# The expert stage of a mixture-of-experts step in native float32, on 32-column token tiles

## The reference

```python
aff = softmax(h @ w_router); gate, idx = top_k(aff, cap)     # per expert: 64 and 16 tokens
xs = h[idx]                                                  # 80 rows of 1024
hid = silu(xs @ w_gate[e]) * (xs @ w_up[e])                  # 1024 -> 2816
out = (hid @ w_down[e]) * gate                               # 2816 -> 1024
acc[idx] += out                                              # scatter-add, then x += gate2 * acc
```

## Time and profile before

| what | us |
|---|---|
| median of 3 runs (lowest, highest) | 2162.31 (2161.64, 2163.51) |
| the profiled execution's own time | 2162.86 |
| its span in the trace | 2161.0 |
| PE busy in the span | 2107.8 (98%) |
| DVE busy | 1598.9 (74%) |
| ACT busy | 1333.8 (62%) |
| DMA over the span | 646.76 MB, 299 GB/s |

### The profile page before, as it was taken

How to read it: one execution, slowest core, us unless ns; L and a number is a source line. 1 busy time by engine, 2 the same in 40 slices (tenths; PEclk the granted TensorE clock), 3 DMA queues, 4 the chain that set the end, 5 groups by cost and what they waited for, 6 DMA issues and landing times.

```text
span 2161.0 us, 28478 instructions
## 1 busy us (share of the span) xinstructions
PE 2107.8 (98%) x11190; PEld 1580.3 (73%) x11190; DVE 1598.9 (74%) x1124; ACT 1333.8 (62%) x953; POOL 252.9 (12%) x233
## 2 busy tenths in 40 slices
PE   8999999999969999999999999999999999999995
PEld 4888899999836676666766666676666767666663
DVE  5555631225568898888888888888888888888885
ACT  5354433123237767777777777777777777777774
POOL 3031136003010101011010101101010010101000
PEclk9999999999979999999999999999999999999998
DMA  8245432222289999999999999999999999999993
GB/s 325 69 152 165 149 111 94 65 77 72 114 323 344 385 383 366 389 359 381 371 386 381 365 390 357 382 378 383 383 362 386 367 377 377 378 385 363 387 374 117
DMA packets 171835, 646.76 MB, mean 299 GB/s; under 512 B 8716, under 2 KB 47880, under 8 KB 171784
## 3 DMA queue, kind: packets, MB, share of 16 engines
q1 hardware_dynamic: 163968, 620.33, 75.6%
q0 software_dynamic: 7632, 25.66, 4.1%
q10 hardware_dynamic: 184, 0.06, 0.0%
HBM read 631.80 MB, written 14.20 MB: 299 GB/s over the span
## 4 chain that ended last, share of the span: by engine, by line
PE 92%; DVE 3%; issue 2%; DMA 1%; ACT 1%; SPq 0%; POOLq 0%; POOL 0%; ACTq 0%; DVEq 0%
PE bank L2067 45%; PE bank L2084 21%; PE bank L1652 16%; PE bank L1786 3%; PE bank L1623 2%; PE bank L1934 2%; DMA a_raw<-in_w_ada_dram 1%; PE bank L1633 1%; PE bank L1634 1%; PE bank L1959 0%; PE bank L2017 0%; PE bank L1870 0%; PE bank L1882 0%; DVE top_i L1492 0%; DMA y_tile<-acc_scratch 0%
## 5 line engine op out<-in xcount | busy, mean ns | idle before, releaser
L1516 DVE TENSOR_TENSOR we_lo<-raw_e,we_hi 128x2816 fp32r<-128x2816 f32 x384 | 1185.4, 3091 | 196.4 <-ACT we_hi L1004 196.2
L1004 ACT ACTIVATE we_hi<-raw_e 128x2816 fp32r<-128x2816 f32 x384 | 980.7, 2559 | 275.1 <-PE bank L2067 200.0
L2067 PE MATMUL bank<-we_hi,xs_hi 128*80 128x512 f32 (+1 forms) x1536 | 409.6, 375 | 1.3 <-DVE xs_lo L1533 1.3
L2067 PE MATMUL bank<-we_hi,xs_lo 128*80 128x512 f32 (+1 forms) x1536 | 409.5, 374 | 0.0
L2067 PE MATMUL bank<-we_lo,xs_hi 128*80 128x512 f32 (+1 forms) x1536 | 408.8, 374 | 0.0
L2067 PEld LDWEIGHTS bank<-we_lo,xs_hi 128*80 128x80 f32 x1536 | 227.1, 148 | 98.6
L2067 PEld LDWEIGHTS bank<-we_hi,xs_lo 128*80 128x80 f32 x1536 | 226.9, 148 | 98.3
L2067 PEld LDWEIGHTS bank<-we_hi,xs_hi 128*80 128x80 f32 x1536 | 224.5, 148 | 98.3 <-issue 1.5
L2084 PE MATMUL bank<-we_hi,hd_hi 128*80 128x512 f32 (+1 forms) x768 | 290.0, 378 | 0.0
L2084 PE MATMUL bank<-we_hi,hd_lo 128*80 128x512 f32 (+1 forms) x768 | 287.2, 374 | 0.0
L2084 PE MATMUL bank<-we_lo,hd_hi 128*80 128x512 f32 (+1 forms) x768 | 286.5, 373 | 0.0
(11 more groups left out here) (310 smaller groups left out, 2178.2 us busy)
## 6 DMA issues: line engine op xcount, KB each, us to landing
raw_e<-in_w_exp_gate_dram SPq DMA_DIRECT2D x128, 1408.0 KB, 10.0
raw_e<-in_w_exp_up_dram SPq DMA_DIRECT2D x128, 1408.0 KB, 9.0
raw_e<-in_w_exp_down_dram SPq DMA_DIRECT2D x96, 1536.0 KB, 8.5
raw_e<-in_w_exp_down_dram SPq DMA_DIRECT2D x32, 1024.0 KB, 10.7
raw_t<-in_w_ada_dram SPq DMA_DIRECT2D x16, 1024.0 KB, 5.2
raw_t<-in_w_in_dram SPq DMA_DIRECT2D x14, 1024.0 KB, 5.1
a_raw<-in_w_ada_dram SPq DMA_DIRECT2D x8, 1024.0 KB, 16.8
raw_t<-in_w_branch_gate_dram SPq DMA_DIRECT2D x8, 1024.0 KB, 5.4
```

Source lines behind the costliest of these rows:

```text
L1004: nc.scalar.activation(we_hi[n % SPLIT_E][:], e_raw(n), ACT.Copy).then_inc(e_hi, 1)
L1516: nc.vector.tensor_tensor(we_lo[n % SPLIT_E][:], e_raw(n), we_hi[n % SPLIT_E][:].bitcast(F32), ALU.subtract)\
L2067: ins = mm(bank[3 * up + c][0:CAP, 0:c1 - c0], a[:, k, :], w[:, kk, c0:c1], start=k == 0 and z == 0, stop=k == KT - 1 and z == 2)
```

## The change

The splits go. Weights are used in native float32, straight from the buffers in which they land. The 80 tokens become three tiles (index x) of 32 columns: two of latent tokens, and one with the 16 context tokens and 16 spare columns, whose index points to 16 spare rows behind the 640 (`h2_dram` and `acc_dram` get 656 rows). A matmul has 32 stationary columns and goes to one of the four 32-column tiles of the array (index c). The four tiles take a quarter of the weight columns each: 352 columns in `gate_up`, 256 in `down`; their results lie in four groups of 32 partitions. So 4 x 3 matmuls cover a block of 128 of the contraction.

With that layout the 32 x 32 block transposes of DVE give the stationary operands: `x_transpose` for the tokens, and one transpose per token tile and half for the hidden values. TensorE transposes and their read-outs go. Gather and scatter move rows of 256 numbers (a quarter of a token's row), 3 x 128 of them in three indirect DMAs each. The raw buffers become a ring of 12, one per piece, freed by `e_used`; 9 pieces are loaded ahead of the first expert. The contraction index is ordered partition first, so a down piece is one run of 12 KB (or 8 KB) per partition. PE and ACT run all 16 experts in one loop. The router stage, the sorting and the tail stay.

The diff, cut to its core:

```diff
             with sp.Fori(0, NE) as e:
                 for n in range(NB):
 
-                    if n < RAW_E and n % PER == 0:
-                        sp.wait_ge(e_free[n // PER], 1)
-                    if n == RAW_E:
-                        sp.wait_ge(e_gath, 16)
-                    half, i = n // RAW_E, n % PER
-                    sp.wait_ge(e_lo, e * NB + n + 1 + (1 if half == 2 and i < PER - 1 else 0))
+                    half, i = n // 8, n % 4
+                    if n == EARLY:
+                        for lt in range(NT):
+                            sp.wait_ge(s_h2w[lt], 16)
+                        sp.wait_ge(e_gath, 16 * NX)
+                    sp.wait_ge(e_used, e * NB + n + 1)
                     if half < 2:
-                        m = (w_exp_gate, w_exp_up)[n % RAW_E // PER]
-                        src = m[0, bass.ds(e, 1), 2 * i * P:2 * (i + 1) * P, half * FH:(half + 1) * FH]\
-                            .rearrange("a (k p) f -> p (a k) f", p=P)
-                        dst = e_raw(n).rearrange("p (k f) -> p k f", f=FH)
+                        m = (w_exp_gate, w_exp_up)[n % 8 // 4]
+                        src = m[0, bass.ds(e, 1)].rearrange("a (p k) f -> p (a k) f", k=KT)\
+                            [:, 2 * i:2 * i + 2, half * FH:(half + 1) * FH]
+                        dst = ring[n % RING][:, 0:2 * FH].rearrange("p (k f) -> p k f", f=FH)
                     else:
-                        g = n % RAW_E // PER
-                        t = FTH * g + DOWN_AT[i]
-                        src = w_exp_down[0, bass.ds(e, 1), t * P:(t + DOWN_N[i]) * P, :]\
-                            .rearrange("a (k p) f -> p (a k) f", p=P)
-                        dst = raw_e[g][:, DOWN_AT[i] * D:(DOWN_AT[i] + DOWN_N[i]) * D].rearrange("p (k f) -> p k f", f=D)
-                    sp.dma_start(dst, src).then_inc(e_landed[n % RAW_E], 16)
-
-            sp.wait_ge(s_acc, 16 * NT + 16 * NE)
+                        g = n % 8 // 4
+                        src = w_exp_down[0, bass.ds(e, 1), g * FH:(g + 1) * FH, :].rearrange("a (p f) d -> p (a f d)", f=FTH)\
+                            [:, DOWN_AT[i] * D:(DOWN_AT[i] + DOWN_N[i]) * D]
+                        dst = ring[n % RING][:, 0:DOWN_N[i] * D]
+                    sp.dma_start(dst, src).then_inc(e_landed[n % RING], 16)
+
...
-
-            def gather():
-                pool.indirect_dma_start(x_rows[:], None, h2_dram, bass.IndirectOffsetOnAxis(idx_gather[:, 0:1], 0))\
-                    .then_inc(e_gath, 16)
+                nc.gpsimd.tensor_tensor(small[:, 62:64], kpow[:, 0:2], kpow[:, 0:2], ALU.add).then_inc(s_hold, 1)
+
+            def gather(idx):
+                for x in range(NX):
+                    pool.indirect_dma_start(x_g[:, x, :], None, h2_rows, bass.IndirectOffsetOnAxis(idx[:, x:x + 1], 0))\
+                        .then_inc(e_gath, 16)
 
             def scatter():
-                pool.indirect_dma_start(acc_dram, bass.IndirectOffsetOnAxis(idx_scatter[:, 0:1], 0), out_rows[:], None,
...
+            def expert(e):
+                for half in range(2):
+                    act.wait_ge(e_used, RING + e * NB + 8 * half + 4)
+                    if half:
+                        act.wait_ge(e_mul, 2 * NX * e + NX)
+                    for x in range(NX):
+                        nc.scalar.activation(silu_g[:, x, :], bank[x][:, 0:FC], ACT.Silu).then_inc(e_silu, 1)
+
+            with act.Fori(0, NE) as e:
+                expert(e)
 
...
+            def x_transpose(e):
+
+                dve.wait_ge(e_gath, 16 * NX * e + 16 * NX)
+                for x in range(NX):
+                    nc.vector.transpose(xs_t[:, x, :].rearrange("p (k t) -> p k t", k=KT),
+                                        x_g[:, x, :].rearrange("p (r k) -> p k r", k=KT)).then_inc(e_xt, 1)
+
+            x_transpose(0)
...
-                        e_split(e + 1, n + SPLIT_E - NB)
+                    nc.vector.tensor_copy(idx_gather[:].unsqueeze(1), idx_all[:, bass.ds(e + 1, 1), :]).then_inc(e_idx, 1)
+                for half in range(2):
+                    dve.wait_ge(e_used, RING + e * NB + 8 * half + 8)
+                    for x in range(NX):
+                        dve.wait_ge(e_silu, 2 * NX * e + NX * half + x + 1)
+                        nc.vector.tensor_tensor(hid[:, x, :], silu_g[:, x, :], bank[3 + x][:, 0:FC], ALU.mult).then_inc(e_mul, 1)
+                    for x in range(NX):
+                        dve.wait_ge(e_mul, 2 * NX * e + NX * half + x + 1)
+                        nc.vector.transpose(hid_t[:, half, :, x * Q:(x + 1) * Q],
+                                            hid[:, x, :].rearrange("p (r f) -> p f r", f=FTH)).then_inc(e_hid, 1)
+                if not last:
+                    x_transpose(e + 1)
+                dve.wait_ge(s_acc, 16 * NT + 16 * NX * e)
+                col = slice(e, e + 1) if isinstance(e, int) else bass.ds(e, 1)
+                nc.vector.tensor_copy(idx_scatter[:].unsqueeze(1), idx_all[:, col, :]).then_inc(e_idx, 1)
+                nc.vector.tensor_copy(gate_cur[:].unsqueeze(1), gate_all[:, col, :]).then_inc(s_idx, 1)
+                dve.wait_ge(s_idx, e + 2)
+                dve.wait_ge(e_used, RING + e * NB + NB)
+                for x in range(NX):
+                    nc.vector.scalar_tensor_tensor(
+                        out=out_rows[:, x, :], in0=bank[6 + x // 2][:, x % 2 * DC:(x % 2 + 1) * DC], scalar=gate_cur[:, x:x + 1],
...
             h2_transpose(4)
             router(4)
             aff_transpose(0, range(NS))
+            def spread(unit, top):
+
+                o = tr(unit)
+                for x in range(NX):
+                    for c in range(4):
+                        ins = mm(o[c * Q:(c + 1) * Q, x * NE:(x + 1) * NE], top[:, x * Q:(x + 1) * Q], ident[0:NE, 0:NE],
+                                 start=True, stop=True)
...
+                    mm(bank[3][0:Q, :], ident[:, 0:Q], ring[0][:, 0:512], start=True, stop=True)
+
+            pe.wait_ge(s_top, CAP // 8 + 1)
+            spread(("ix", 0, 0), top_f)
+            spread(("ga", 0, 0), top_v)
             pe.wait_ge(wo_read, 2 * NT)
...
+            def gate_up(e, n):
+
+                half, up, i = n // 8, n % 8 // 4, n % 4
+                w = ring[n % RING][:, 0:2 * FH].rearrange("p (k f) -> p k f", f=FH)
+                if half and i == 0:
+                    if up:
+                        pe.wait_ge(e_hid, 2 * NX * e + NX)
+                    else:
+                        pe.wait_ge(e_silu, 2 * NX * e + NX)
                 for kk in range(2):
                     k = 2 * i + kk
+                    for x in range(NX):
+                        for c in range(4):
+                            ins = mm(bank[3 * up + x][c * Q:(c + 1) * Q, 0:FC], xs_t[:, x, k * Q:(k + 1) * Q],
+                                     w[:, kk, c * FC:(c + 1) * FC], start=k == 0, stop=k == KT - 1)
                 ins.then_inc(e_used, 1)
 
             def down(e, n):
 
+                half, i = n % 8 // 4, n % 4
+                w = ring[n % RING][:, 0:DOWN_N[i] * D].rearrange("p (f d) -> p f d", d=D)
+                if i == 0:
+                    pe.wait_ge(e_hid, 2 * NX * e + NX * half + NX)
+                    if half == 0:
+                        pe.wait_ge(e_out, NX * e + NX)
+                for j in range(DOWN_N[i]):
+                    f = DOWN_AT[i] + j
+                    for x in range(NX):
+                        for c in range(4):
+                            ins = mm(bank[6 + x // 2][c * Q:(c + 1) * Q, x % 2 * DC:(x % 2 + 1) * DC],
+                                     hid_t[:, half, f, x * Q:(x + 1) * Q], w[:, j, c * DC:(c + 1) * DC],
+                                     start=half == 0 and f == 0 and x != 1, stop=half == 1 and f == FTH - 1, skip_group_check=True)
                 ins.then_inc(e_used, 1)
 
+            def expert(e):
+                pe.wait_ge(e_xt, NX * e + NX)
                 for n in range(NB):
+                    pe.wait_ge(e_landed[n % RING], 16 * (NB // RING) * e + 16 * (n // RING + 1))
+                    if n < 16:
+                        gate_up(e, n)
                     else:
                         down(e, n)
+
+            with pe.Fori(0, NE) as e:
+                expert(e)
+
```

More of the change, by code:

```diff
@@ L309, in build @@
         assert dead + 25856 + 512 <= 229344 - base
[L311 to L314, removed]
+        ring = [at(f"ring{i}", o, [P, PIECE]) for i, o in enumerate(
+            (0, 12288, 24576, 61440, 73728, 86016, 98304, 147456, 159744, 110592, 122880, 135168))]
         def wt(m, wide, extra, out):
@@ L1062, in _ @@
-            e_split(0, 0)
-            for lt in range(NT):
-                act.wait_ge(s_h2w[lt], 16)
-            e_split(0, 1)
-            e_split(0, 2)
-            act.wait_ge(s_idx, 2)
-            x_hi(0, 0)
-            x_hi(0, 1)
-            def expert(e, last):
-                for n in range(NB):
-                    if n in TR_AFTER:
```

(45 more changed lines are left out.)

250 lines of the change are left out of this document (66 added, 184 removed).

## The result

The changed kernel takes 2141.33 us (median of 4 runs, 2139.67 to 2142.75) against 2162.18 us before on the same chip: a ratio of 0.990, 95% interval 0.9885 to 0.992. It is faster, as forecast, but by 21 us and not by 109. The forecast of 2053 and its range to 2105 missed.

A forecast was written before the change was run, and what follows sets the result against it. PE was taken to bound the kernel, DMA just behind: start 639.6 + passes 1365 + loop turns 20 + tail 27.0 = 2051.6, plus 1.9 us outside the span, 2053.5; forecast 2053 us, range 2030 to 2105.

The forecast's parts named there:

- PE's passes: Expert stage on PE: gate and up 56.9 us plus down 28.5, together 85.3 us per expert, 1365 us for 16.
- The turn of the loop: End of PE's loop body: 10 instruction blocks may not stay held; a fetch wait of 1.3 us, x 15 = 20 us.
- the nearer landing: At the loop's turn: the instruction fetch was priced as a small transfer's landing of 2.2 us.
- The lead of 0.9 us: At the loop's turn: PE's sequencer is 33 records ahead, 4 passes or 0.9 us, taken off the fetch wait.
- the upper bound, 4.4: At the loop's turn: longest wait per turn, a small transfer's 5.3 us landing less PE's queued work.
- The DMA side: Expert stage's transfers: weights 83.8 us plus gather and scatter 3.4, so 87.2 us per expert, just behind PE.
- Start and tail: Before and after the expert stage: start at 639.6 us, and 27.0 us from the last matmul to the span's end.
- No stall: Rival at the loop's turn: PE doesn't wait for instructions, 2033 to 2045 us; chance 23%.
- Supply at 62 ns per matmul: Rival in PE's instruction supply: a down pass takes 248 ns, 4.2 us more per expert, 2121 us; chance 4%.
- tiles that don't overlap: Rival in PE's passes: each load delays its matmul, 0.11 us more per pass, about 2600 us; chance 3%.
- rows by number: Rival in gather and scatter: small rows cost 13.5 us, so 97.3 us per expert, 2190 us; chance 4%.
- The DMA share near 1: Sign that the forecast is right: DMA engines' busy share near 1 at 400 GB/s or more.

The follow-up runs named there:

- The written-out kernel: The changed kernel with PE's 16 experts written out one after the other instead of in a loop: 2040.76 us, ratio to before 0.943.
- the DMA engines at 26 GB/s: The changed kernel with each weight transfer from the second expert on bringing only 64 columns of its piece, PE's instructions the same: 2086.94 us.
- the one tried here, 1824 records: The changed kernel with 8 ring buffers instead of 12 and an inner PE loop over the halves of gate and up: 2146.84 us.
- the kernels that were held: The changed kernel with 8 buffers, the inner loop and part of the third token tile's down product left out, 1472 or 1632 records: 2018.7 and 2018.2 us.

## Why the prediction was wrong

- **PE's passes: right.** Sixteen times 85.3 us. The written-out kernel has this period with no gap in PE. The gain of 8.6 us per expert over the 93.95 of before was there.
- **The turn of the loop: the step that failed.** "I take the nearer landing, 2.2 us, less 0.9 = 1.3, x 15 = 20 us". It is 7.1 us, x 15 = 107. That the ten blocks would not stay was foreseen. The price was wrong in three places. A branch with the DMA engines at 26 GB/s takes 3.6 us and not 2.2. The full weight transfers make it 6.0; neither landing in the earlier trace rows was one of a fetch behind streaming weights. And the clock's fall was in no term at all, 1.8 us. The lead of 0.9 us was right: 6.0 - 0.9 = 5.1. Even the upper bound, 4.4, lay below the idle time alone, since its landing of 5.3 us was no bound for a fetch. 107 - 20 = 87 of the 88 us missed are here. The first expert's half clock, in no term either, is 1.7 more; start and tail give back 1.
- **The DMA side: right.** 85.6 us per expert where it is the limit and no instructions are fetched, 86.7 and 88.0 at the end of the written-out kernel, where I had 87.2. It never limits the changed kernel; PE's waits show no landing. Small rows don't cost by number: gather and scatter are 3.9% of 1255 us, 3.6 us per expert, where by bytes I had 3.4 and by number 13.5.
- **Start and tail: right.** 639.1 against 639.6, and 26.4 us (2138.4 - 2112.0) against 27.0.
- **The rivals.** "No stall" (2033 to 2045) is what the written-out kernel measures, 2040.8. Supply at 62 ns per matmul, tiles that don't overlap and rows by number are out: PE passes its quads without a gap. The DMA share near 1, which I named as a sign, tells little: it reads 0.99 at 386 GB/s with PE the limit and 1.02 at 411.

What stays open: what decides whether the clock falls behind 2.2 to 2.8 us of idle time, why a fetch at a turn takes 3.6 us with the DMA engines at 26 GB/s (one block's journey, or several in a row), and why 1632 records are held and 1728 are not. That blocks read ahead take part of the room would fit the 1.7 blocks fetched in excess at each turn, but this was only argued.

## What to carry to other kernels

Count the records in a PE loop's body before you shorten its matmuls: finer tiles mean more of them, and past a room that ended between 1632 and 1728 here, each turn costs a fetch that short matmuls no longer hide. Above that, write the loop out, or bring its code under that room with an inner loop; the one tried here, 1824 records, was not short enough, and the kernels that were held leave out work. Once the stall is gone, look at the next limit: the DMA engines' 85.6 us per expert are already above PE's 85.3. Price a stall in PE as its idle time plus the passes at half clock behind it, and price a small fetch in the load under which it will run; the instruction rows among the DMA queues show at once whether a loop is held.

The written-out kernel, 2040.8 us, beats both: 5.7% under the kernel before.

## What the runs showed of the hardware

- A taken branch back over 930, 768, 1472 or 1632 records takes at most 0.25 us; over 1728 or more, 6.0 to 6.2 us at the median with weights streaming at 370 to 400 GB/s; over 2592 at 26 GB/s, 3.6 us. It doesn't grow with the body (1728, 2592 and 5184 records: 6.1, 6.0, 6.1).
- Straight-line code of 10.2 blocks per 85.3 us is fetched with no stall (the written-out kernel).
- Native float32 on four column tiles goes at full pace for 1040 us without a gap (638.6 to 1680 us of the written-out kernel): one quad of 352 columns each every 0.295 us.
- TensorE's clock after idle time, by what gate and up take beyond 56.98 us: 1.7 to 1.8 us behind 3.9 to 5.1 us idle, 2.0 and 2.9 behind 5.5 and 6.4, 2.1 in the median behind 11.1 to 12.9; behind 2.2 to 2.8 us, 1.4 to 1.7 at 7 of 15 turns and nothing at 8.
- Transfers of 34.6 MB per expert with gathers and scatters beside them take 85.6 us when nothing holds them back, 413 GB/s.
